# A two-block transformer on one core: the modulation's sums over k tiles on VectorE, and five low parts from GpSimd to VectorE

## The reference

```
def swiglu(h, w_gate, w_up, w_down):                 # D_FF = 2816 = 11 x 256, twice (DEPTH = 2)
    return (jax.nn.silu(h @ w_gate) * (h @ w_up)) @ w_down

for l in range(DEPTH):                               # first block
    ...                                              # mixer, cross attention
    h = rms_norm(x, pre_ffn_g[l])
    x = x + rms_norm(swiglu(h, w_gate[l], w_up[l], w_down[l]), post_ffn_g[l])

mod = jax.nn.silu(c) @ w_ada[0] + b_ada[0]           # second block: 1024 -> 6144
shift1, scale1, gate1, shift2, scale2, gate2 = jnp.split(mod, 6, axis=-1)
h = modulate(rms_norm_2(x, norm_pre_mix[0]), shift1, scale1)      # h * (1 + scale) + shift
...                                                  # attention, gating, then 16 experts
```

## Time and profile before

| | |
|---|---|
| time, median of 3 runs (lowest, highest) | 2523.73 us (2508.76, 2529.51) |
| the profiled execution's own time, its span | 2525.98 us, 2524.2 us |
| busy in the span: PE, DVE, ACT, POOL | 1941.9, 740.6, 529.3, 105.6 us (77%, 29%, 21%, 4%) |
| layer 0: mixer and cross, then FFN | to about 317, then to 537 us |
| layer 1: mixer and cross, then FFN | to about 832, then to 1057 us |
| second block: attention and gating, then the experts | to about 1246, then to the end |

### The profile page before, as it was taken

One profiled execution on the slowest core, in us unless ns is written; L12 is line 12 of the kernel. 1 busy time (PEld: TensorE's weight loads), 2 busy tenths in 40 slices (PEclk: granted clock), 3 DMA queues, 4 the chain that ended last, 5 costly groups with the idle time before them and its releaser, 6 DMA issues.

```text
span 2524.2 us, 29737 instructions
## 1 busy us (share of the span) xinstructions
PE 1941.9 (77%) x13188; PEld 1254.4 (50%) x13188; DVE 740.6 (29%) x1083; ACT 529.3 (21%) x800; POOL 105.6 (4%) x145
## 2 busy tenths in 40 slices
PE   8999799989999899788766666666666667665665
PEld 7769698879798788677522122112111122111121
DVE  4545544456454444554411000100011010110012
ACT  5435433345254333333200000000000000000000
POOL 2100100011000100110000000000000000000000
PEclk9879999999799899996887788877788677877887
DMA  8215357654153466632699999999999999999996
GB/s 268 93 59 176 117 192 230 204 168 152 36 189 129 156 212 222 209 101 92 288 429 431 428 427 431 429 428 428 430 430 428 429 430 428 430 429 429 430 429 281
DMA packets 171072, 739.86 MB, mean 293 GB/s; under 512 B 6672, under 2 KB 133136, under 8 KB 146240
## 3 DMA queue, kind: packets, MB, share of 16 engines
q1 hardware_dynamic: 168592, 731.27, 73.2%
q0 software_dynamic: 2352, 6.69, 0.8%
HBM read 736.88 MB, written 1.05 MB: 292 GB/s over the span
## 4 chain that ended last, share of the span: by engine, by line
DMA 45%; PE 43%; DVE 6%; ACT 3%; issue 2%; POOL 0%; SPq 0%; DVEq 0%; ACTq 0%
PE PS L312 43%; DMA WB<-in_w_down 23%; DMA WB<-in_w_up 22%; DVE WL L1371 2%; ACT WH L912 1%; DVE C L1363 1%; DVE X L1366 1%; DVE S L1366 0%; PE PS L502 0%; DMA W<-in_w_in 0%; ACT C L980 0%; DVE N L1437 0%; DVE T L1363 0%; ACT S L942 0%; DVE S L1363 0%
## 5 line engine op out<-in xcount | busy, mean ns | idle before, releaser
L312 PE MATMUL PS<-WB,XS 128*32 128x352 f32 x3072 | 363.7, 635 | 212.3 <-DMA WB<-in_w_up 125.5
L1371 DVE TENSOR_TENSOR WL<-W,WH 128x2048 fp32r<-128x2048 f32 x136 | 313.8, 2308 | 242.6 <-ACT WH L912 242.6
L312 PE MATMUL PS<-WB,S 128*32 128x512 f32 x1408 | 268.5, 762 | 150.4 <-issue 77.7
L312 PEld LDWEIGHTS PS<-WB,XS 128*32 128x32 f32 x3072 | 116.2, 141 | 456.1 <-issue 177.8
L312 PE MATMUL PS<-HTh,WH 128*128 128x256 f32 x1064 | 307.1, 289 | 5.4 <-DVE HTl L1366 2.5
L912 ACT ACTIVATE WH<-W 128x2048 fp32r<-128x2048 f32 x141 | 269.0, 1908 | 178.8 <-PE PS L312 171.1
L312 PE MATMUL PS<-HTl,WH 128*128 128x256 f32 x1064 | 300.9, 283 | 0.0
L312 PE MATMUL PS<-HTh,WL 128*128 128x256 f32 x1064 | 300.8, 283 | 0.0
L1366 DVE SCALAR_TENSOR_TENSOR S<-S,PS 128x352 f32<-128x352 f32 (+1 forms) x110 | 63.4, 588 | 795.9 <-ACT S L1336 756.9
L312 PEld LDWEIGHTS PS<-WB,S 128*32 128x32 f32 x1408 | 71.1, 127 | 337.4 <-issue 224.6
L312 PEld LDWEIGHTS PS<-HTh,WH 128*128 128x128 f32 x1064 | 203.7, 191 | 8.8 <-DVE WL L1371 3.2
(11 more groups left out here) (268 smaller groups left out, 2189.7 us busy)
## 6 DMA issues: line engine op xcount, KB each, us to landing
WB<-in_w_down SPq DMA_DIRECT2D x64, 2816.0 KB, 36.1
WB<-in_w_gate SPq DMA_DIRECT2D x48, 2816.0 KB, 35.5
WB<-in_w_up SPq DMA_DIRECT2D x48, 2816.0 KB, 35.9
C<-in_w_gate SPq DMA_DIRECT2D x16, 2816.0 KB, 36.2
C<-in_w_up SPq DMA_DIRECT2D x16, 2816.0 KB, 37.2
W<-in_w_in SPq DMA_DIRECT2D x31, 1024.0 KB, 5.9
W<-in_w_ada SPq DMA_DIRECT2D x24, 1024.0 KB, 5.4
W<-in_w_gate SPq DMA_DIRECT2D x22, 1024.0 KB, 7.8
```

What stands on the lines that cost most here:

```text
L312: return e.matmul(o, l, r, start=start, stop=stop, skip_group_check=True)
L1371: e.tensor_tensor(M.WL[i][:, :], M.W[:, 2048 * (m % NW):2048 * (m % NW) + 2048], M.WH[i][:, :].bitcast(F32), ALU.subtract).then_inc(*up("l ...
```

## The change

The products of silu(c) with `w_ada` are summed over the eight k tiles by VectorE: one TENSOR_SCALAR and seven SCALAR_TENSOR_TENSORs (STTs) over 128 x 256 values, each after the one before, into one of two accumulators `AD`. TensorE keeps only the sum over the 128 partitions, with a tile of ones. ScalarE's copy, `CB` and the products of `fill_ada` are gone. VectorE does the first four operations of unit n at the place where it added the bias before, and the other four one iteration later, after the low part of the next up unit. TensorE makes the sum of unit n - 1 where it did all of unit n before. The slot of a modulation unit is now free after VectorE's last operation on it. The modulation's sections come in another order (`ADA`), and the unit that was the second at n = 5 now stands between the last two down units. The bias is added with one operation instead of up to two. GpSimd's `low` is gone: the five units keep their early high part, and VectorE makes their low part in its usual `ahead`, after the norm.

```diff
+ADA = [n for n in range(24) if n // 4 not in (2, 5)] + [n for n in range(24) if n // 4 in (2, 5)]
...
@@ tensor_program
-        for kk in range(2):
-            for q in range(4):
-                ins = mm(ps[32 * q:32 * q + 32, 0:256], M.CB[:, 4 * kk + q, :], u[:, 4 * kk + q, :], kk == 0, kk == 1)
-        ins.then_inc(*up("unit", m))
-        same(("ada4", n), ("unit", m))
-        e.wait_ge(*at("ada_sb", n))
...
+        ps, acc, ones = take(("ada", n)), M.AD[i % 2], M.CST[:, C_ONES:C_ONES + 128]
+        e.wait_ge(*at("ada_acc", n))
+        if sec in (2, 5):
+            ins = mm(ps[:, 0:256], ones, acc, True, True)
...
+            for k in range(2):
+                ins = mm(ps[:, k:k + 1], acc[:, 128 * k:128 * k + 128], ones[:, 0:1], True, True)
+        ins.then_inc(*up("ada_sum", n))
...
             if n > 1:
                 down(n - 2)
-            for _ in range(2 if n == 5 else 1):
-                fill_ada(C.ada.pop(0))
+            if n:
+                ada_sum(mods[n - 1])
+            ada_unit(mods[n])
         down(9)
+        ada_sum(mods[10])
+        ada_unit(mods[11])
         down(10)
...
@@ scalar_program, ada
-        e.activation(M.AD, PS[:, 4 + i, 0:256], ACT.Copy).then_inc(*up("ada_sb", n))
...
@@ vector_program
-    done = set(C.early)
+    done = set()
...
+    def modulation(i):
+        n, m = C.ada_units[i]
+        acc, w = M.AD[i % 2], M.W[:, 2048 * (m % NW):2048 * (m % NW) + 2048].rearrange("p (k n) -> p k n", k=8)
+        e.wait_ge(*at(f"w{m % NW}", m))
+        if i > 1:
+            e.wait_ge(*at("ada_sum", ADA[i - 2]))
...
+        ts(acc, w[:, 0, :], K["cs"][:, 0:1], None, ALU.mult).then_inc(*step())
+        for k in range(1, 8):
+            if k == 4:
+                yield
+            own()
+            stt(acc, w[:, k, :], K["cs"][:, k:k + 1], acc, ALU.mult, ALU.add).then_inc(*(up("ada_acc", n) if k == 7 else step()))
+        same(("unit", m), ("ada_acc", n))
...
         for n in range(11):
             A, i = M.A[n % 2], n % 4
             unit()
+            if job:
+                run_all(job)
             unit()
...
             if n > 1:
                 unit()
-            for _ in range(2 if n == 5 else 1):
-                ada(C.ada.pop(0))
+            job = modulation(12 * l + n)
+            next(job)
+            if n:
+                ada_sum(mods[n - 1])
+            ada_unit()
...
         unit()
-        unit()
+        run_all(job)
+        job = modulation(12 * l + 11)
+        next(job)
+        ada_sum(mods[10])
+        ada_unit()
+        unit()
+        run_all(job)
...
@@ gpsimd_program
-            e.tensor_tensor(M.WL[i][:, :], M.W[:, 2048 * (m % NW):2048 * (m % NW) + 2048], M.WH[i][:, :].bitcast(F32),
-                            ALU.subtract).then_inc(*up("pool_low", m))
-            same(("low", m), ("pool_low", m))
```

More of the change, by code:

```diff
@@ L198, in memory @@
     C1, N1 = sb("C1", [128, NCONST + 512 + 3584]), sb("N1", [128, 4096])
-    M.CST, M.CB = C1[:, 0:NCONST], C1[:, NCONST:NCONST + 256].rearrange("p (a b) -> p a b", a=8)
-    M.AD, J1 = C1[:, NCONST + 256:NCONST + 512], C1[:, NCONST + 512:NCONST + 512 + 3584]
+    M.CST, M.AD = C1[:, 0:NCONST], [C1[:, NCONST + 256 * i:NCONST + 256 + 256 * i] for i in range(2)]
+    J1 = C1[:, NCONST + 512:NCONST + 512 + 3584]
     M.ID = M.CST[:, 0:128]
@@ L653, in ffn @@
                 down(n - 2)
-            for _ in range(2 if n == 5 else 1):
-                fill_ada(C.ada.pop(0))
+            if n:
+                ada_sum(mods[n - 1])
+            ada_unit(mods[n])
         down(9)
+        ada_sum(mods[10])
+        ada_unit(mods[11])
         down(10)
-    C.ada = list(range(24))
+        ada_sum(mods[11])
+    C.ada_units = []
     for l in range(2):
@@ L970, in post_squares, with ada_unit @@
                     *up("ysq", *y, t, h))
-    def ada(n):
+    def ada_unit():
         nonlocal here
@@ L1454, in ada @@
             e.wait_ge(*at("ga"))
-            e.tensor_tensor(o, ps[:, 256:512], o, ALU.add).then_inc(*freed("ada", n))
-        else:
[L1457 to L1465, removed]
+            e.tensor_tensor(o, ps[:, 0:256], o, ALU.add).then_inc(*freed("ada", n))
+            return
+        if sec < 2:
+            s = 8 * sec + 2 * j
+            o, b, i = K["MT"][:, s:s + 2], par("b_ada", s, 2), ps[:, 0:2]
+        else:
+            o, b, i = (v[32 * j:32 * j + 32] for v in (K["MT"][:, 8 * sec - 8:8 * sec], par("b_ada", 8 * sec, 8), ps[:, 0:8]))
+        stt(o, i, 1.0 if sec in (1, 4) else 0.0, b, ALU.add, ALU.add).then_inc(*freed("ada", n))
     def parameters():
@@ L1493, in parameters @@
         own()
-        ts(K["cs"], K["cs"], 0.5, None, ALU.mult).then_inc(*step())
-        own()
-        e.tensor_copy(M.CB[:, :, :], K["cs"].unsqueeze(2).broadcast_to([128, 8, 32])).then_inc(*up("cb"))
+        ts(K["cs"], K["cs"], 0.5, None, ALU.mult).then_inc(*up("cs"))
         yield
@@ L1759, in ffn @@
     def ffn(l):
+        mods = ADA[12 * l:12 * l + 12]
+        job = None
         for n in range(11):
@@ L2020, in gpsimd_program @@
     up, at, M, K, D = C.sig.up, C.sig.at, C.M, C.M.small, C.D
[L2021 to L2029, removed]
-            e.tensor_tensor(M.WL[i][:, :], M.W[:, 2048 * (m % NW):2048 * (m % NW) + 2048], M.WH[i][:, :].bitcast(F32),
-                            ALU.subtract).then_inc(*up("pool_low", m))
-            same(("low", m), ("pool_low", m))
+    free = C.free
     def power(o, i, n):
@@ L2208, in __init__ @@
         self.M, self.D, self.sig = M, D, sig
-        self.banks, self.units, self.early, self.ada = Banks(), Units(), set(), []
+        self.banks, self.units, self.ada_units = Banks(), Units(), []
     def free(self, *use):
```

45 lines of the change are left out of this document (15 added, 30 removed).

## The result

The kernel after takes 2576.0 us in the median (2575.2 to 2578.6), the kernel before 2525.7 beside it (2508.8 to 2529.5): a ratio of 1.021, 95% interval 1.017 to 1.026. The change makes the kernel 50 us slower; 2577 was predicted.

The account below looks back on a forecast made before the run. TensorE bounds the loop before; after, a 22.1 us loop through SP's load order does. 2526.0 + 30.1 + 25.1 (FFNs) + 15.0 (behind them) - 16.6 (diagonals) = 2579.6, 2577 us as median; range 2545 to 2608.

Parts of the forecast that it names:

- The loop: FFN iteration: ada load, gate load behind it, VectorE's and ScalarE's chain, next ada load; 22.1 us against TensorE's 17.7.
- One sign: FFN loop: PE would show two gaps an iteration, ahead of gate and of up.
- A step on VectorE: Modulation sum: TENSOR_SCALAR 0.44 us, each STT 0.48, bounds 0.44 to 0.51; each half 1.9 us.
- the prediction's sign: Modulation sum: VectorE's STTs would be 0.48 us apart.
- Length of an FFN: End of up 0 to last matmul: 234.7 us, so +30.1 us in layer 0 and +25.1 in layer 1.
- Behind an FFN: Post-norm begins 5.6 us after TensorE's end; the block moves by 7.5 us, +15.0 for two.
- A(10): Moment the accumulator of modulation unit 10 is done, put 6.3 us before TensorE's end of the FFN.
- The diagonals: Two diagonal tiles at four later norms fall from 4.63 us to 0.48: -16.6 us.
- The low part on VectorE: After the norms: 2.29 us on VectorE, hidden behind a 5.7 us TensorE unit, costing nothing.
- rival 3: FFN loops: the clock stays low through whole loops, about +230 us, 2800 us; chance 6 in 100.
- The range and the sum: Whole kernel: terms sum to 2579.6 us, 2577 as median; range 2545 to 2608, from ends of 2527 and 2613.
- ahead of the first FFN: Start to first hidden product of FFN 0: predicted change -4.15 us.

Follow-up runs that it names:

- Three experiments: Kernel after with, respectively, gate load ahead of ada load (2494.6 us), second half ahead of up's low part (2521.2), first TENSOR_SCALAR made three times (2593.8).
- more work on TensorE: Kernel after, with three more products of the same size after each of TensorE's sums over partitions: 2585.3 us, ratio to before 1.023.
- the changed list alone: Kernel after, with each w_ada load one place later in SP's list, behind the gate or down load: 2494.6 us, again 2492.0.

## Why the prediction was right, and where its terms were off

- *The loop.* Predicted 22.1 us, measured 21.8. Term by term from 426.72: the gate load 0.4 later, its landing 7.9, high part 1.9, low part 2.2, first half 1.8, the chain from the bias to the second half 5.45, second half 2.1. Three experiments move it by the amount that the sum gives: -4.1 (down to TensorE's 17.7), -3.3 and +0.8. The wait that closes it was found in SP's list, not on a compute engine. One sign was read wrong: two gaps of TensorE an iteration were forecast, and in most there is one, ahead of the gate unit. In the two iterations of layer 0 with a second gap (402.8 and 512.2) the gate unit between them runs at a clock of 1.00; in the seven others its mean clock is 0.58 to 0.77, it takes longer, and the low part of up is ready when it ends. The three second gaps of layer 1 fit the same way.
- *A step on VectorE.* An STT takes 0.485 us in the median of 168, but two of them start 0.52 us apart, not 0.48 as the prediction's sign had it, and above its bound of 0.51. From the TENSOR_SCALAR to the first STT it is 0.38. The two errors cancel: a first half is 1.8 us and a second 2.1, where 1.9 each was put. The page VectorE: DVE Perf Modes of the Trainium skill (TRN2 errata) gives 0.33; the trace disagrees.
- *Length of an FFN.* From the end of up 0, 0.2 ahead of the first hidden product (331.4 and 871.9), to the last matmul (567.3 and 1108.4) it is 235.9 and 236.5 us, where 234.7 was predicted: +31.3 and +26.9 against +30.1 and +25.1.
- *Behind an FFN.* This term was mis-sized. Predicted 7.5 us each, measured 3.6 and 5.4: the post-norm begins 1.7 and 3.5 us after TensorE's end, not 5.6. From A(10) to the post-norm it is 11.5 and 11.4 us, close to the 11.9 of the sum. What was off is TensorE's end: A(10) was put 6.3 us ahead of it, by a down unit of 5.7, and lies 9.8 us ahead in layer 0 (557.5) and 7.9 in layer 1 (1100.5). The window in layer 0 has the reason:

```profile
557.00:562.00 5.00, 4.39 (x24) 3.75 (x25) 2.35 (x6) 0.00 (x0) 0.00 (x0) 0.60 0.68 200
```

  Right after its gap TensorE runs the sum and down 10 at a granted clock of 0.60, so it ends late, and the FFN takes from the tail what it adds itself. The sum of both terms, +34.9 and +32.4 against +37.6 and +32.6, was close because the two terms share this error with opposite signs.
- *The diagonals.* 0.48 us at all five norms, as predicted; -16.6 by the rows. The low part on VectorE was hidden, as predicted. The Trainium skill's GPSIMD Engine Reference (Key points) has the two engines share SBUF interfaces when VectorE is in a two-port mode; the experiment that only delays GpSimd agrees, and no run here shows in which mode VectorE was.
- *The clock (rival 3).* It does fall behind the new gaps, and comes back:

```profile
349.00:357.00 8.00, 5.81 (x28) 5.81 (x29) 6.09 (x10) 2.72 (x3) 0.00 (x0) 0.57 0.36 136
...
426.72:448.51 21.79, 19.11 (x117) 18.05 (x116) 12.48 (x15) 5.58 (x6) 0.00 (x0) 0.84 0.58 193
```

  The mean over the iteration shown is 0.84 and over the FFNs 0.91 and 0.94. TensorE is then busy for 19.1 us of the 21.8 instead of 17.7, and the loop doesn't feel it, as the forecast had it. What it had not: 88 to 108 us, in the mixer of layer 0, has a clock of 0.83 after the change and 1.00 before, with TensorE busy throughout in both, and the same work there takes 3.0 us longer. The change edits nothing in that stretch; why the clock fell is not shown. That this piece also varies by 5.5 us between two profiles of one kernel speaks against putting it down to the change.
- *The range and the sum.* The low end of the range, 2545, was called half the way down from 2577 to 2527; that would be 2552. The result doesn't depend on it. The sum was 2579.6 for a profiled span of 2526.0 with what lies around it; the profiled run after took 2578.6. The errors by part, measured less predicted, are -6.0 for the two tails, +3.0 for the two FFNs, +3.0 ahead of the first FFN and -1.4 between them. They nearly cancel, so that the total came within 1 us is luck; the parts say how well the mechanism was known.

## What to carry over

When work moves from one engine to another, ask which buffer comes free later by it, whose load waits for that buffer, and what stands behind that load in the queue. A queue in order turns a slot that is late for one load into a delay of the next engine's food; here 72 us in two FFNs lay in the order of two loads, and the cure costs no instruction. An engine that is a third busy can still set the time by the place of four operations in its list.

## What was not expected of the hardware

- An fp32 TENSOR_SCALAR of 128 x 128 on VectorE that starts 0.14 us behind GpSimd's TENSOR_TENSOR of 128 x 2048 ends with it (4.43 us beside 4.49), while two such tiles take 0.48 where GpSimd starts 0.56 us after them. This tile pays what is left of the longer operation, not a share of it. A TENSOR_TENSOR with both inputs in SBUF was held in the same way (1.17 us for 0.42, once). STTs with an input in PSUM are not held: 0.48 us each, beside GpSimd and alone.
- A gate load of 1 MB that is issued 0.41 us behind another takes 7.8 to 8.1 us in some iterations and 8.8 to 9.5 in others, in one run (more work on TensorE) whose SP issues look alike.
- In the mixer of layer 1 the clock stays at 0.50 for some 30 us with TensorE busy for all of them, in most kernels here but in neither profile of the changed list alone; that is worth 12 to 15 us, more than several of the edits that were to be measured. Times of kernels that differ in it must be compared stage by stage.
